# Thirty projection tiles beside the attention: one 512-column matmul over both parts of the activations instead of two of 256, and a fold on VectorE

## The reference, cut to what matters

```python
h = rms_norm(x, norm_g)
proj = h @ w_in
aq, ak, av, ag, rs, rg, xq, xg, mg = _split(proj, ...)
...
y_a = windowed_gqa(q, k, va, attn_sink) * jax.nn.silu(ag)
...
prev = jnp.pad(p, ((0, 0), (1, 0), (0, 0)))[:, :-1]
nxt = jnp.pad(p, ((0, 0), (0, 1), (0, 0)))[:, 1:]
p = p + mu * (0.5 * (prev + nxt) - p)        # on rs, the input of the rwkv branch
...
y_x = memory_xattn(qx, km, vm) * jax.nn.silu(xg)
```

## Time and profile before

| | |
|---|---|
| median of 3 runs | 3511.65 us (3508.11 to 3512.32) |
| the profiled execution | 3509.05 us |
| its span on the core | 3506.7 us |
| TensorE busy with matmuls | 3442.9 us, 98% |
| TensorE weight loads | 3105.5 us, 89% |
| VectorE busy | 2452.9 us, 70% |
| ScalarE busy | 1644.0 us, 47% |
| mean granted clock of TensorE | 0.996 |

### The profile page before, as it was taken

One profiled execution on the slowest core, in us unless ns is written; L12 is line 12 of the kernel. 1 busy time (PEld: TensorE's weight loads), 2 busy tenths in 40 slices (PEclk: granted clock), 3 DMA queues, 4 the chain that ended last, 5 costly groups with the idle time before them and its releaser, 6 DMA issues.

```text
span 3506.7 us, 73526 instructions
## 1 busy us (share of the span) xinstructions
PE 3442.9 (98%) x27134; PEld 3105.5 (89%) x27134; DVE 2452.9 (70%) x3551; ACT 1644.0 (47%) x2252; POOL 287.8 (8%) x358
## 2 busy tenths in 40 slices
PE   8999999999999999999999999999999999999998
PEld 8999888899988899988888888888899988888886
DVE  6986777866776577877657565677766865656566
ACT  6456433444544435754534353444444643434344
POOL 5000234200020000002000000020000200000002
PEclk9999999999999999999999999999999999999999
DMA  7444222255655555555555655556554555656564
GB/s 254 161 156 142 89 87 87 86 177 185 213 191 185 189 169 181 169 166 189 189 186 187 194 182 192 186 186 191 168 168 158 179 180 183 194 185 192 181 195 139
DMA packets 164985, 604.03 MB, mean 172 GB/s; under 512 B 18336, under 2 KB 18464, under 8 KB 164560
## 3 DMA queue, kind: packets, MB, share of 16 engines
q1 hardware_dynamic: 163584, 596.16, 52.7%
q10 hardware_dynamic: 1040, 3.16, 0.2%
q0 software_dynamic: 192, 2.23, 0.2%
HBM read 599.38 MB, written 2.10 MB: 172 GB/s over the span
## 4 chain that ended last, share of the span: by engine, by line
PE 89%; DVE 7%; ACT 2%; issue 1%; POOL 0%; DMA 0%; ACTq 0%; DVEq 0%; POOLq 0%
PE bank L366 40%; PE bank L369 20%; PE bank L345 9%; PE bank L346 8%; PE bank L347 8%; PE bank L1362 4%; DVE w_lo L334 3%; ACT w_hi L325 1%; POOL x_norm_acc L466 0%; DVE nrm_kk L1039 0%; DVE X L2979 0%; PE bank L848 0%; DVE X L2983 0%; PE bank L731 0%; DVE sq_at L744 0%
## 5 line engine op out<-in xcount | busy, mean ns | idle before, releaser
L325 ACT ACTIVATE w_hi<-raw 128x1024 fp32r<-128x1024 f32 x1126 | 1157.7, 1053 | 809.7 <-PE bank L369 564.6
L334 DVE TENSOR_TENSOR w_lo<-raw,w_hi 128x1024 fp32r<-128x1024 f32 x1126 | 1351.0, 1236 | 100.0 <-ACT w_hi L325 99.7
L366 PE MATMUL bank<-hid,w_hi 128*128 128x512 f32 x2048 | 643.4, 395 | 0.0
L366 PE MATMUL bank<-u,w_hi 128*128 128x512 f32 x1536 | 484.4, 397 | 0.0
L369 PEld LDWEIGHTS bank<-hid,w_lo 128*128 128x128 f32 x2048 | 384.7, 188 | 90.9
L366 PE MATMUL bank<-xh,w_hi 128*128 128x512 f32 x1312 | 413.5, 397 | 3.0 <-DVE w_lo L334 3.0
L369 PE MATMUL bank<-hid,w_lo 128*128 128x256 f32 x2048 | 402.3, 278 | 0.0
L369 PEld LDWEIGHTS bank<-u,w_lo 128*128 128x128 f32 x1536 | 289.6, 189 | 69.2
L345 PE MATMUL bank<-hx,w_hi 128*128 128x256 f32 x1088 | 329.0, 302 | 12.6 <-DVE w_lo L334 12.6
L366 PEld LDWEIGHTS bank<-hid,w_hi 128*128 128x128 f32 x2048 | 311.9, 189 | 0.1
L347 PE MATMUL bank<-hx,w_lo 128*128 128x256 f32 x1088 | 308.3, 283 | 0.5 <-issue 0.5
(11 more groups left out here) (484 smaller groups left out, 5987.1 us busy)
## 6 DMA issues: line engine op xcount, KB each, us to landing
raw<-stream SPq DMA_DIRECT2D x1126, 512.0 KB, 4.0
x_raw<-xT SPq DMA_DIRECT2D x4, 512.0 KB, 7.4
mem_raw<-memT ACTq DMA_DIRECT2D x4, 512.0 KB, 9.6
x_res<-xT POOLq DMA_DIRECT2D x1, 2048.0 KB, 8.5
out<-X SPq DMA_DIRECT2D x3, 512.0 KB, 2.7
cst<-consts SPq DMA_DIRECT2D x1, 1504.0 KB, 13.5
out<-X SPq DMA_DIRECT2D x2, 256.0 KB, 2.2
w_sb<-w ACTq DMA_DIRECT2D x1, 384.0 KB, 5.0
```

The costliest lines, as they stand in the source:

```text
L325: nc.scalar.activation(w_hi[:, slot], raw[:, slot], ACT.Copy).then_inc(hi_ready, 1)
L334: nc.vector.tensor_tensor(w_lo[:, slot], raw[:, slot], w_hi[:, slot].bitcast(F), ALU.subtract).then_inc(lo_ready, 1)
L366: nc.tensor.matmul(bank[:], w_hi[:, slot, i], both(moving, kt), start=kt == 0, stop=False)
```

## The change

TensorE takes the thirty tiles with `wide_tile` instead of `full_tile`. VectorE, when the tile is done, first adds the two halves of the bank into `fold[tile.parity]` with a `tensor_reduce`, waits for its own semaphore `beside_fold`, and takes `fold` where it took the first half of the bank. TensorE's wait before tile k is no longer on L628 or L636 of tile k-2 but on its fold.

```diff
+        beside_fold = sem("beside_fold")
+
         def dve_beside(v, tiles):
             for k in tiles:
                 tile, kind, m, n = beside(k)
                 tile_done(v, tile)
-                psum = banks[tile.parity][:, 0:T]
+                psum = fold[tile.parity][:]
+                nc.vector.tensor_reduce(psum, banks[tile.parity][:].rearrange("p (a t) -> p t a", a=2), AX.X, ALU.add).then_inc(beside_fold, 1)
+                v.wait_ge(beside_fold, k + 1)
                 if kind == "silu":
...
                     pe.wait_ge(mem_out, COUNT["mem_kv"] - 1 + k)
                 else:
 
-                    _, kind, _, n = beside(k - 2)
-                    pe.wait_ge(agate_pre if kind == "silu" else shift_copied, n + 1)
-                full_tile(pe, tile, hx)
+                    pe.wait_ge(beside_fold, k - 1)
+                wide_tile(pe, tile, hx)
```

## The result

The changed kernel takes 3513.44 us (median of 20 runs, 3510.05 to 3518.72), the kernel before 3508.73 (20 runs beside them, 3505.53 to 3512.32). The ratio is 1.0015, with a 95% interval of 1.0009 to 1.0021: 4.7 us slower. 3515.8 was forecast with a range of 3508 to 3521, and no change beyond 0.2% as the likeliest case. By the means of the same runs the changed kernel is 5.6 us slower (3514.44 against 3508.86), since its slower executions lie farther out. The profiled execution of the changed kernel took 3516.91 us, its span 3514.6 against 3506.7: +7.9, which is more than the median shows.

A forecast was written before the change was run, and what follows sets the result against it. TensorE was taken to bound the kernel (98% busy), VectorE at places in the changed stage. Folds 8.64 minus short tiles 3.23 minus early pr 1.24 made +4.2 on 3511.65: 3515.8 us, range 3508 to 3521.

The forecast's parts named there:

- The gain of a tile: On TensorE a wide tile takes 5.57 us against 5.76 for a full one: 0.19 us, 5.7 at most for thirty.
- Rival (d): In the changed stage a wide tile gains only 0.04 us: +6.7 us, 3518.4 us; chance 0.04.
- The fold: On VectorE each tile's added reduction costs 0.72 us, 21.6 us of work over thirty tiles.
- the sum: Whole stage: 12 folds on the path, 8.64 us, minus short tiles 3.23, minus early pr 1.24: +4.2 us.
- Stretch 1: Up to the transposes of unit 0: VectorE has no idle time, folds of tiles 0 to 3 and 5 count, +3.6 us.
- Stretch 2: Transposes of unit 0 to unit 4: twelve tiles at TensorE's pace, -2.3 us, standing +1.3, pr margin 0.32 left.
- rival (b): Transposes of units 1 to 4: VectorE becomes the bound, each unit loses 0.53 us, +8.7, 3520.4 us; chance 0.09.
- Stretch 3: To the transposes of unit 5, no third tile: VectorE's chain sets pr, TensorE waits 0.7 us; +0.4, standing +1.7.
- Stretch 4: Units 5 to 9: second tiles' folds are on the chain, silu tiles' folds hide in VectorE's wait; +2.5 us.
- The clock: Longer waits before tile 6 and unit 9's transposes may halve the clock: 1.2 us covered at the first, +1.2 at the second.
- Rival (a): The clock also falls behind the wait before unit 9's transposes: 3517.0 us; chance 0.15.
- Rival (c): VectorE's folds hide and TensorE's gain on all thirty tiles stands: 3506.0 us; chance 0.12 with half-way forms.

The follow-up runs named there:

- the kernel with extra matmuls: Changed kernel plus unread 512-column matmuls in four waits: before tile 6, kk of unit 6, unit 9's transposes and first rwkv product; 3513.57 us, ratio 1.0011.

## Why the prediction was right

**The time and its base.** +4.2 was forecast, +4.7 was measured. The forecast of 3515.8 was 2.4 above the measured median because it was laid on the median of the three runs shown, 3511.65, and the kernel before has a median of 3508.73 over 20 runs. The base was off by 2.9 us and the change by 0.5, so the base was the greater error. The interval of the change is 3 to 7 us, so the medians confirm its size only roughly; the places in the timeline do it better.

**The gain of a tile.** 0.19 us from the merge; in place it is (20.60 - 20.09)/3 = 0.17. Rival (d), 0.04, is out. The formula from which the prediction worked out 0.04 is given by the Trainium skill ("TensorE: Matmul & The Clock Gate", section "Back-to-back issue gap") for the gap of one isolated matmul. The same section says that it does not hold for a stream with a weight load ahead of each matmul, and this condition is missing in the prediction. The trace disagrees with the formula for such a stream, and the measured pair in the merge decides.

**The fold.** 684 ns in the mean, 0.69 in the merge. Without wide tiles the folds cost 8.0 us of time in the median; the sum had 8.64 - 1.24 = 7.4 for them. At the product of that trace it is 8.26, of which about 1 us is the half clock ahead of unit 0.

**Stretch 1, +3.60.** Measured +3.59, and the wait ahead of tile 6 3.89 against at most 4.0. The half clock behind it was foreseen, and that the wait for `pr` covers it. The cover is 1.47 us in the kernel with extra matmuls, and it was wholly used in the changed kernel, where the transposes started without a wait. That it was just enough is in part luck: with full tiles the same half clock was on the path, by 1 us.

**Stretch 2.** No wait in the transposes of units 1 to 4, so rival (b) is out. VectorE's last work ahead of the transposes of unit 2:

```profile
242.54 1.14 DVE L939 TENSOR_SCALAR pr<-pr,rd 128x256 f32<-128x256 f32 x4
```

It ends at 243.68 and the transposes start at 244.00: the margin is 0.32 us, as forecast. The standing was +1.55 instead of +1.3: twelve tiles at 0.17 instead of 0.19.

**Stretch 3, +1.7.** Measured +1.94 with a wait of 0.57 (forecast 0.7); VectorE's `w_lo` waited 1.38 us for ScalarE, as the chain through the silu tile's `w_hi` wanted it. It carries stretch 2's 0.2.

**Stretch 4, the mis-sized term.** At full clock (extra matmuls at all four) the transposes of units 7, 8 and 9 were late by 2.88, 3.59 and 4.29: 0.70 a unit, not 0.53. What the prediction had wrong here was that the folds of the silu tiles lie in VectorE's wait for the second tile. On VectorE they do. But ScalarE waits for the silu tile too. ScalarE in unit 8 of the kernel with extra matmuls, from the silu to the weight split:

```profile
333.63 0.42 ACT L616 ACTIVATE sg<-sa 128x256 f32<-128x256 f32 x1 [3.69 <-DVE sa L632]
...
339.62 2.01 ACT L325 ACTIVATE w_hi<-raw 128x1024 fp32r<-128x1024 f32 x2
```

The silu starts 333.63 - 331.79 = 1.84 us behind the transposes; before it was 1.11 (330.02 - 328.91). ScalarE goes on without a stop to the pair of `w_hi`, so this starts 7.83 us behind the transposes instead of 7.11. VectorE's rows in the same unit:

```profile
338.06 0.69 DVE L626 TENSOR_REDUCE fold<-bank 128x256 f32<-128x512 f32 x1 [1.81 <-PE bank L369]
338.79 0.43 DVE L640 TENSOR_TENSOR pad<-fold,x_norm_rstd 128x256 f32<-128x256 f32 x1
...
340.71 2.36 DVE L334 TENSOR_TENSOR w_lo<-raw,w_hi 128x1024 fp32r<-128x1024 f32 x2
```

From `pad` to `w_lo` are now 1.92 us, before 1.78 (337.13 - 335.35): `w_lo` waits a little for ScalarE's first `w_hi`, which ends near 340.67. The tile gives 0.17, the fold takes 0.73, ScalarE's lateness 0.14: 0.70. (This is read from the rows of one unit; no run moved the silu tile's fold alone.) The last step was the other way: from unit 9 to `y9` +0.33 instead of 0.53, and from `y9` to the product -0.24, which is the extra matmuls' doing and not the change's. The last pair of `w_lo`, the kernel before first, then the one with extra matmuls and its `y9`, each with GpSimd's copy for the rwkv stage:

```profile
367.87 2.65 DVE L334 TENSOR_TENSOR w_lo<-raw,w_hi 128x1024 fp32r<-128x1024 f32 x2
...
368.05 1.39 POOL L1141 COPY v_pair<-rkv 128x256 f32 x1
```

```profile
371.96 0.62 POOL L1154 COPY v_pair<-rkv 128x256 f32 x1
...
372.78 2.35 DVE L334 TENSOR_TENSOR w_lo<-raw,w_hi 128x1024 fp32r<-128x1024 f32 x2
375.05 0.41 DVE L957 TENSOR_TENSOR sg<-bank,sg 128x256 f32<-128x256 f32 x1
```

Before, the two ran at the same time and both took longer; now the copy is over first, and `w_lo` takes 0.30 us less. The twelve kernels divide cleanly: in the six where tile 29 has no fold the copy takes 1.39 us and the pair of `w_lo` 2.65 (2.64 once), in the six where it has one 0.62 and 2.35. (That the overlap is the cause is read from these rows, no experiment was made on it.) So two misses of stretch 4 cancel in part, which is luck: 4.62 at `y9`, 4.56 at the product like against like, 4.17 forecast.

**The clock.** Left out of the sum, with a chance of 0.15 and 1.2 us for a fall behind unit 9. The fall happened in the profiled execution, at unit 9 and at a place that the forecast did not name: the wait at `kk` of unit 6, which grew from 0.97 to 1.69. The step that was mis-sized was "+1.2": behind unit 9 it is 1.6 to 2.9 us, since the half clock stayed for some 3 us in some traces and 7 in others, and together with unit 6 it is 4.4. Rival (a), 3517.0, is close to the profiled execution of 3516.91 only by chance: laid on the profiled execution of the kernel before, as the forecast's 3513.2 was, it would be 3514.4. The median shows next to nothing of the clock, the mean some 1.7 us, so the forecast's choice held for the median that it was made for.

**Rival (c).** All folds hidden would be 3 us faster by the kernel without folds, not 5.7, even so. It is out: the folds without wide tiles are slower, ratio 1.0013 to 1.0031, and the transposes of unit 0 are 3.59 us late.

## What to carry to other kernels

A form that takes work from TensorE and gives some to VectorE is worth its price only where TensorE is the last to arrive: here the eleven tiles of the three-tile units gained 1.65 us at the transposes behind them, and the six tiles at the start, ahead of which VectorE never stops, lost 3.6 (no median here is sharp enough to show the gain). Look for two consumers before calling an added operation hidden: the folds of the silu tiles were free on VectorE and late for ScalarE. And when a trace shows a longer step than the medians of many runs, look at the granted clock behind the waits that have grown before looking for a mechanism, compare the means and the mean clock of all runs beside the medians, and put the same extra matmuls into the kernel before as into the changed one.

## What the runs showed of the hardware

- The granted clock does not go by the wait alone. At `kk` of unit 6 it fell behind a wait of 1.69 us in two kernels and stayed behind the same wait in two others, 1.70 with tiles 6 to 29 wide and 1.69 with folds alone. Ahead of unit 9 it stayed behind 2.34 us in the kernel before, fell behind 2.34 with tiles 7 to 17 wide, and stayed behind 3.07 with folds alone. At 2816 us of the kernel before it fell at a wait of 1.96 us, and it stayed at the same place and wait in the changed kernel. What else decides it was not found.
- A few matmuls without use in the wait kept the clock at 1.00 at every place where they were put, and cost nothing that the medians show, as they end ahead of the wait's own end: the waits that are left are 0.22 to 0.95 us.
- At half clock the wide tile is as good as halved in speed: in the changed kernel two contraction tiles, which take 5.57/8 = 0.70 us at full clock, stand 1.27 us apart behind unit 9 (L366 at 367.81 and at 369.08 us).
